# LRU stage with combined neighbour blocks and spread tiles, and a rebuilt first norm, first head and end

## What is computed

```python
h = rmsnorm(x, norm_mix)
q, k, v, g_ret, x_lru, y_lru, g_a, g_b = split(h @ w_in)
o, S_new = retention(rope(q), rope(k), v, S_ret)              # 4 heads, 256 x 512
ret_branch = (silu(g_ret) * groupnorm(o)) @ w_ret_out
xc = causal_conv(x_lru, conv_buf, conv_w, conv_b)             # width 1280, 4 taps
r, i = sigmoid(blockdiag(xc, w_a) + b_a), sigmoid(blockdiag(xc, w_x) + b_x)   # 16 blocks of 80
a = exp(-8 * r * softplus(-lam)); u = sqrt(1 - a * a) * i * xc
hl = scan(h = a * h + u)
lru_branch = (gelu(y_lru) * hl) @ w_lru_out
x = x + (sigmoid(g_a) * ret_branch + sigmoid(g_b) * lru_branch) @ w_o
x = x + (silu(h2 @ w_gate) * (h2 @ w_up)) @ w_down            # h2 = rmsnorm(x, norm_ffn), width 2816
```

## Time and profile before

| | |
|---|---|
| median of 3 runs | 2510.93 us (2508.16 to 2512.69) |
| profiled execution | 2510.63 us, its span 2508.8 us |
| TensorE busy | 2430.4 us, 97% |
| VectorE / ScalarE / GpSimd busy | 1191.4 / 606.9 / 1724.1 us |
| mean granted TensorE clock | 0.989 |
| moved by DMA | 298.6 MB, mean 119 GB/s |

### The profile page before, as it was taken

One profiled execution on the slowest core, in us unless ns is written; L12 is line 12 of the kernel. 1 busy time (PEld: TensorE's weight loads), 2 busy tenths in 40 slices (PEclk: granted clock), 3 DMA queues, 4 the chain that ended last, 5 costly groups with the idle time before them and its releaser, 6 DMA issues.

```text
span 2508.8 us, 53186 instructions
## 1 busy us (share of the span) xinstructions
PE 2430.4 (97%) x19604; PEld 2374.5 (95%) x19604; DVE 1191.4 (47%) x1613; ACT 606.9 (24%) x869; POOL 1724.1 (69%) x1993
## 2 busy tenths in 40 slices
PE   7999999999989999999989999999999899999997
PEld 7899999999989999999988999999999899999997
DVE  6554555477463532022256554545874645221223
ACT  2313121325361211011113132222353612100111
POOL 5365757488787877777754757565887777777774
PEclk9999999999999999999999999999999999999998
DMA  4445545422223222322235546352222332223222
GB/s 162 166 154 173 173 169 180 144 91 89 87 82 90 93 92 85 94 97 85 92 126 195 179 148 208 137 192 107 91 91 84 79 94 92 92 88 97 92 83 85
DMA packets 120224, 298.61 MB, mean 119 GB/s; under 512 B 19136, under 2 KB 19648, under 8 KB 120064
## 3 DMA queue, kind: packets, MB, share of 16 engines
q1 hardware_dynamic: 60480, 199.78, 24.8%
q10 hardware_dynamic: 59584, 96.56, 11.3%
HBM read 255.92 MB, written 40.38 MB: 118 GB/s over the span
## 4 chain that ended last, share of the span: by engine, by line
PE 86%; DVE 5%; ACT 2%; DMA 2%; issue 2%; DVEq 2%; ACTq 1%; POOL 0%; POOLq 0%; SPq 0%
PE banks L369 79%; PE banks L535 2%; PE banks L497 1%; DVE scratch L878 1%; PE banks L551 1%; PE banks L527 1%; DMA scratch<-in_sret 1%; DVE scratch L1080 1%; PE banks L514 1%; DMA w_raw<-in_wstream 1%; DVE rinv L697 0%; ACT scratch L1306 0%; DVE scratch L980 0%; DVE scratch L1062 0%; PE banks L454 0%
## 5 line engine op out<-in xcount | busy, mean ns | idle before, releaser
L355 POOL TENSOR_TENSOR w_low<-w_raw,w_high 128x256 fp32r<-128x256 f32 (+1 forms) x1568 | 1287.3, 852 | 62.2 <-issue 0.8
L350 POOL TENSOR_SCALAR w_high<-w_raw 128x1024 fp32r<-128x1024 f32 (+3 forms) x420 | 437.6, 1042 | 699.1 <-PE banks L369 671.0
L369 PE MATMUL banks<-x_high,w_high 128*128 128x260 f32 x4096 | 835.8, 285 | 44.8 <-DVE scratch L1102 15.6
L369 PE MATMUL banks<-x_high,w_low 128*128 128x260 f32 x4096 | 828.5, 284 | 0.0
L369 PE MATMUL banks<-x_low,w_high 128*128 128x260 f32 x4096 | 826.8, 284 | 0.0
L369 PEld LDWEIGHTS banks<-x_high,w_high 128*128 128x128 f32 x4096 | 635.4, 190 | 55.6 <-issue 47.2
L369 PE MATMUL banks<-split_scratch,w_high 128*128 128x260 f32 x4000 | 643.5, 283 | 5.4 <-DVE split_scratch L1091 5.4
L369 PEld LDWEIGHTS banks<-x_high,w_low 128*128 128x128 f32 x4096 | 634.7, 189 | 0.0
L369 PEld LDWEIGHTS banks<-x_low,w_high 128*128 128x128 f32 x4096 | 634.2, 189 | 0.0
L369 PEld LDWEIGHTS banks<-split_scratch,w_high 128*128 128x128 f32 x4000 | 548.9, 189 | 6.4 <-issue 6.0
L369 PE MATMUL banks<-split_scratch,w_low 128*128 128x260 f32 x2000 | 403.2, 283 | 0.0
(11 more groups left out here) (157 smaller groups left out, 1773.7 us busy)
## 6 DMA issues: line engine op xcount, KB each, us to landing
w_raw<-in_wstream SPq DMA_DIRECT2D x268, 512.0 KB, 3.5
scratch<-in_sret ACTq DMA_DIRECT2D x64, 512.0 KB, 7.3
out_ret_s<-scratch ACTq DMA_DIRECT2D x64, 512.0 KB, 3.4
w_raw<-in_wstream SPq DMA_DIRECT2D x64, 384.0 KB, 3.0
w_raw<-in_wstream SPq DMA_DIRECT2D x40, 448.0 KB, 3.2
scratch<-v_rows ACTq DMA_DIRECT2D x64, 256.0 KB, 4.5
w_raw<-in_wstream SPq DMA_DIRECT2D x48, 320.0 KB, 2.8
out_ret_p<-scratch ACTq DMA_DIRECT2D x8, 512.0 KB, 2.8
```

What stands on the lines that cost most here:

```text
L350: pool.tensor_scalar(WH[:, j, w], WR[:, j, w], 1.0, 0.0, ALU.mult, ALU.add)
L355: m = pool.tensor_tensor(WL[:, j, p], WR[:, j, p], WH[:, j, p].bitcast(F32), ALU.subtract)
L369: m = pe.matmul(out, wt[:, w, blk * P:(blk + 1) * P], x[xi], start=first and n == 0, stop=last and n == 2)
```

## The change

- Neighbour blocks: for an inner tile t the inputs of the upper half's neighbour (the lower half of tile t + 1) and of the lower half's neighbour (the upper half of t - 1) are copied into one tile XN (`neighbours`, ScalarE, four copies of 64 partitions), and the host combines the two weight blocks into one (`near`). A gate tile of t = 1, 2, 3 has 2 blocks in place of 3, and a y unit always 6.
- Second group: y(1,1) moves ahead of the 8 output tiles, y(1,2) into their middle; two more buffers for gated tiles (GLX); the orders of VectorE and ScalarE are written anew to match.
- First norm: X is loaded first, the gain is read from NRM, the square root's table is loaded at the start, ACC is cleared by GpSimd, all scalings and low parts stand ahead of half of the squares, and layer 0's norm sums come after the second tile. In each layer's first head the third tile goes into the fourth PSUM place.
- First head: `decays` in two parts, `conv_of_states` later, states and products earlier.
- The layer loop is unrolled on every engine; `norm_root` comes first in a layer; cos and sin of layer 1 are loaded after the last head of layer 0; the square root's table is loaded before the norm loops.
- End: the last norm makes no high and low parts, and its sums wait for the squares alone.

```diff
-YG_UNIT = [(MT + 2 * len(BAND[t])) // 2 for t in range(GT)]
...
+YG_UNIT = [(MT + 2 * 2) // 2] * GT
...
-             + [("y", 1, 0), ("ga", 0, GT)] + [("out", 0, m) for m in range(MT)]
-             + [("y", 1, t) for t in range(1, GT)] + [("ga", 0, m) for m in range(GT + 1, MT)])
+             + [("y", 1, 0), ("ga", 0, GT), ("y", 1, 1)] + [("out", 0, m) for m in range(MT // 2)]
+             + [("y", 1, 2)] + [("out", 0, m) for m in range(MT // 2, MT)]
+             + [("y", 1, 3), ("y", 1, 4)] + [("ga", 0, m) for m in range(GT + 1, MT)])
...
-            with sp.Fori(0, DEPTH) as layer:
+            for layer in range(DEPTH):
...
             pool.memset(ONES[:], 1.0).then_inc(s["ones_ok"], 1)
+            pool.memset(ACC[:], 0.0).then_inc(s["ones_ok"], 1)
...
                     if first:
                         whole(ub, 0, tb, 0, XH, XL, s["x_low_s"], layer * (2 * MT))
-                        norm_sums()
+                        if layer:
+                            norm_sums(2 * layer)
                         whole(ub, 1, tb, 1, XH, XL)
+                        if layer == 0:
+                            norm_sums(0)
                     else:
                         whole(ub, 0, tb, 0, XH, XL)
                         whole(ub, 1, tb, 1, XH, XL)
                         samples_by_channel(hh - 1)
                         for e in range(VT - 1):
                             out_by_channel(hh - 1, e)
-                    whole(ub, 2, tb, 2, XH, XL)
+
+                    whole(ub, KT, tb, KT, XH, XL, place=FIRST_K if first else None)
...
+                    q = spread(ub0, u, YG_UNIT[t], tb0, idx, [pairs(XH, XL, k) for k in range(MT)], 0)
+                    if t in INNER:
+                        n = g * len(INNER) + t - 1
+                        pe.wait_ge(s["xn_full"], layer * (GROUPS * len(INNER)) + (n + 1))
+                        xs = [pairs(XCH, XCL, t), pairs(XNH, XNL, n % 2)]
+                    else:
+                        pe.wait_ge(s["xc_low"], layer * LT + (g * GT + BAND[t][-1] + 1))
+                        xs = [pairs(XCH, XCL, k) for k in BAND[t]]
                     for w in range(2):
-                        q = spread(ub0, u, YG_UNIT[t], tb0, idx + 1 + w, XCH, XCL, BAND[t], q)
+                        q = spread(ub0, u, YG_UNIT[t], tb0, idx + 1 + w, xs, q)
...
                 y_gates(1, 0)
                 gate_a(GT)
+                y_gates(1, 1)
                 pe.wait_ge(s["gl_low"], layer * LT + GT)
-                for m_ in range(MT):
+                for m_ in range(MT // 2):
                     lru_out(ub0, B_OUT[m_], tb0, C_OUT[m_])
-                for t in range(1, GT):
-                    y_gates(1, t)
+                y_gates(1, 2)
+                for m_ in range(MT // 2, MT):
+                    lru_out(ub0, B_OUT[m_], tb0, C_OUT[m_])
+                y_gates(1, 3)
+                y_gates(1, 4)
                 for m_ in range(GT + 1, MT):
...
             for m in range(MT):
-                dve.wait_ge(s["x_high_s"], m + 1)
-                norm_low(X[:, m, :], XH[:, m, :], XL[:, m, :], GAIN[:, m:m + 1], m % 2, m == 0
-                         ).then_inc(s["x_low_s"], 1)
-                dve.drain()
-            with dve.Fori(0, DEPTH) as layer:
+                first_low(m)
+                if m > MT // 2:
+                    first_sum(m - MT // 2)
+            for m in range(MT // 2, MT):
+                first_sum(m)
+            dve.wait_ge(s["ones_ok"], 2)
+            dve.wait_ge(s["setup_ld"], 16 * 3)
+            for layer in range(DEPTH):
...
                     v_tile(1)
-                    if not first:
+                    if first:
+                        decays(0)
+                    else:
                         og_split(hh - 1)
                         dve.drain()
                     dve.tensor_copy(GNC[:], CUR[:, bass.ds(head * VT + PC_GN, VT)])
                     for e in range(2, VT):
                         v_tile(e)
-                        if first:
-                            (decays if e == 2 else conv_of_states)()
+                        if first and e == 2:
+                            decays(1)
                     aux(N_VS)
                     ts(OT[TT], AUX[:, BANK[N_VS], :], 1.0, None, ALU.mult).then_inc(aux_free[BANK[N_VS]], 1)
                     dve.drain().then_inc(s["vs_full"], 1)
+                    if first:
+                        conv_of_states()
                     if not first:
                         for m_ in range(MT):
...
                         dve.drain()
                         gate(0)
+                        new_state(1)
                     else:
                         score_low(0)
                         score_low(1)
...
                         k_low(i)
                     v_low(0)
                     if first:
-                        new_state(0)
+                        new_state(2)
                     gate(1)
                     for j in range(1, TT):
                         v_low(j)
                     if first:
-                        for n in range(1, SRING):
-                            new_state(n)
+                        new_state(3)
                     gate(2)
...
-                read_y(1, 0)
-                use_gates(1, 0)
                 scan(GT - 1)
                 conv_low(1, GT - 1)
                 gated_low(GT - 1)
+                read_y(1, 0)
+                use_gates(1, 0)
                 one_less_a2(GT)
                 use_ga(GT - 1)
                 read_ga(GT)
-                for m_ in range(MT):
-                    read_out(m_)
-                for t in range(1, GT):
-                    read_y(1, t)
-                    use_gates(1, t)
-                    scan(GT + t - 1)
-                    if t == 1:
-                        use_ga(GT)
-                    one_less_a2(GT + t)
-                    gated_low(GT + t - 1)
-                scan(LT - 1)
-                gated_low(LT - 1)
-                for m_ in range(GT + 1, MT):
-                    read_ga(m_)
-                for m_ in range(GT + 1, MT):
-                    use_ga(m_)
+
+                scan(GT)
+                gated_low(GT)
+                use_ga(GT)
+                read_y(1, 1)
+                use_gates(1, 1)
+                read_out(0)
+                one_less_a2(GT + 1)
+                read_out(1)
+
+                scan(GT + 1)
+                read_out(2)
+                gated_low(GT + 1)
+                read_out(3)
+                read_y(1, 2)
+                use_gates(1, 2)
+                read_out(4)
+                one_less_a2(GT + 2)
+                read_out(5)
+
+                scan(GT + 2)
+                read_out(6)
+                read_out(7)
+                gated_low(GT + 2)
+                read_y(1, 3)
+                use_gates(1, 3)
+                one_less_a2(GT + 3)
+
+                read_y(1, 4)
+                scan(GT + 3)
+                use_gates(1, 4)
+                one_less_a2(GT + 4)
+                read_ga(GT + 1)
+                gated_low(GT + 3)
+                scan(GT + 4)
+                gated_low(GT + 4)
+                read_ga(GT + 2)
+                use_ga(GT + 1)
+                use_ga(GT + 2)
...
+            def load_x(m):
+                act.dma_start(X[:, m, :], xt[:, m, :]).then_inc(x_ld[m], 16)
+
+            load_x(0)
+            act.dma_start(NRM[:], norms).then_inc(s["norm_ld"], 16)
+            for m in range(1, MT):
+                load_x(m)
+            act.wait_ge(s["boot"], 1)
+            A(TOUCH, EPST, ACT.Sqrt)
+            act.wait_ge(s["norm_ld"], 16)
+
+            def first_square(m):
+                A(SQ0[:, m, :] if m else SSQ, X[:, m, :], ACT.Square).then_inc(s["x_sq"], 1)
+
+            for m in range(MT):
+                act.wait_ge(x_ld[m], 16)
+                A(XH[:, m, :], X[:, m, :], copy, scale=NRM[:, 0, m:m + 1]).then_inc(s["x_high_s"], 1)
+                if m >= MT // 2:
+                    first_square(m - MT // 2)
+            for m in range(MT // 2, MT):
+                first_square(m)
+
...
                     if first:
+                        product(0)
+                        product(1)
                         silu(0)
                         for i in range(TT // 2):
                             k_high(i)
                         v_high(0)
-                        product(0)
-                        product(1)
-                        silu(1)
-                        for j in range(1, TT):
-                            v_high(j)
                         keep(0)
                         product(2)
                         keep(1)
                         product(3)
+                        silu(1)
+                        for j in range(1, TT):
+                            v_high(j)
                         keep(2)
                         keep(3)
                         product(4)
                         product(5)
                         silu(2)
```

(42 more changed lines are left out.)

208 lines of the change are left out of this document (121 added, 87 removed).

## The result

| | before | after |
|---|---|---|
| median | 2511.08 us (4 runs, 2508.16 to 2512.69) | 2468.35 us (4 runs, 2467.48 to 2471.05) |
| ratio | | 0.983, interval [0.9816, 0.985] |
| span of the profiled run | 2508.8 us | 2465.9 us |
| mean granted clock | 0.989 | 0.993 |

The change gains 42.7 us; 61.4 were forecast, and the time lies 0.35 us above the range of 2437 to 2468. The sign was right, the size was not.

What follows compares the result with a forecast made beforehand. TensorE, busy 97%, bounds the kernel; only fewer matmuls or holes help. Terms 3.0 + 30.2 + 6.8 + 5.8 + 6.8 + 7.2 + 1.6 = 61.4 us give 2449 us; forecast 2437 to 2458 (chance 0.70), outer bound 2468.

Steps and rivals of the forecast that it cites:

- What bounds, and the price of a hole: Whole kernel: TensorE's pace bounds, 0.72 us a block; a hole also slows the clock, 1.7 us for each.
- Fewer blocks and first group: LRU first group: 12 blocks fewer save 4.3 us a layer, less 2.8 for a new hole at y(0,1): net 1.5.
- Second group: LRU second group through merge: reordering y tiles and outputs gains 16.0 us in layer 0, 14.2 in layer 1.
- the 1.0 that I charged to GpSimd: LRU second group: 1.0 us charged for GpSimd's low pieces taking longer beside the chain, with one unit's lead.
- The stores: Merge: four small state stores beside it delay a weight load; 1.3 us charged (0 to 3).
- The heads: Loop over heads 1 to 3 in each layer: the prediction's sum held no term for it.
- The third rival: Unrolled layers: engines fetch new code, TensorE stalls 2.11 us at each fetch, some 25 a layer: 2555 us; chance 0.03.
- First norm: Kernel start: X loaded first, first matmul near 8 us, norm sums earlier; gain 6.8 us (3.5 to 9.5).
- First heads, layer change, end: First heads gain 5.8 and 6.8 us, the unrolled layer change 7.2, the last norm's sums 1.6.
- The chain (1): End of LRU second group: the ScalarE-VectorE chain still decides, holes of about 5 us a layer: 2459 us; chance 0.14.
- GpSimd (2): LRU second group: GpSimd becomes the bound, 11 us a layer: 2471 us; chance 0.08.

Runs made afterwards that it cites:

- the kernel with 20 waits: Kernel after with 20 already fulfilled TensorE waits (10 instructions) ahead of each layer's head loop: 2460.11 us, one execution.
- The run with 90 waits: Kernel after with 90 already fulfilled TensorE waits (45 instructions) ahead of each layer's head loop: 2452.47 us, one execution.
- The experiment: Kernel after with four of the residual's eight loads issued by ScalarE between its first splits: 2466.07 us, one execution.
- the run with three blocks: Kernel after plus 90 fulfilled waits ahead of each head loop, with inner tiles' gates made of three blocks again: 2467.98 us, one execution.
- heads written out: Kernel after with TensorE's loop over heads 1 to 3 written out in each layer: 2459.62 us, ratio to before 0.980.
- stores late: Kernel after with ScalarE's four small stores moved from ahead of merge to the feed-forward stage's start: 2457.35 us, ratio to before 0.979.
- both starts: Kernel after with four of eight residual loads issued by GpSimd (2471.86 us), or by ScalarE between its first splits (2466.07 us).
- 45 and 90 waits: Kernel after with 45 or 90 fulfilled TensorE waits (22 or 45 instructions) ahead of each head loop: 2454.6 and 2452.47 us.
- layer loop: Kernel after with only TensorE's two layers a loop again, layer 1's norm sums one tile later: 2462.9 us, ratio to before 0.981.

## Why the prediction was wrong

**What bounds, and the price of a hole.** It held: TensorE's pace, the block of 0.72 us, and that a hole is paid twice. But whether the clock falls is not the hole's size alone: 2.28 us at 555.67 brought half clock in after, and 2.29 us at 547.98 in the kernel with 20 waits did not. My 1.7 us each, or half of it, was a fair mean. The times of one kernel lie 2 to 7 us apart, and its executions with the longer times tend to show the lower mean clock. The run with 90 waits gained more than its holes for this reason.

**Fewer blocks and first group.** Right within about a microsecond. Four half-height copies start 0.65 us apart and not 0.54, so four take 2.6 us, the upper bound; a copy of 64 partitions takes 0.64 us, as long as one of 128. The hole was 2.28 us in layer 0, with half clock behind it, and 1.08 us in layer 1, with none, where 2.0 stood.

**Second group.** The hand-made order held: merge starts 91.7 us after y(1,0) where 91 was forecast. The hole of 1 to 2 us in the second output tile didn't come; instead TensorE waits for `w_low` (0.52, 0.30 and 0.41 us at 647, 677 and 697) and 0.10 at 665, 1.3 us together, near the 1.0 that I charged to GpSimd.

**The stores.** Here a term was mis-sized: 1.3 us a layer, against 6.1 and 4.3 us in the traces, 10.4 together, and 11.0 for both in the run without them there. I had the right row, 9.2 us for a load, and saw that the merge would now run at full speed beside it, but took the delay of the load for hidden by two buffers. I ought to have worked out the lead: the load of the earlier trace rows is some 6 us late, GpSimd comes from the second group with one unit of lead (3.6 to 4.3 us of TensorE's work), and the 2 us or more that are left bring half clock behind them. With the 10.4 us of the traces in the place of 2.6 the sum would have given 2457.

**The heads.** This is the step that failed: I gave the loop over the heads no term at all, and it cost 10.9 us, more than half of the miss. The third rival had the mechanism, that an engine without its next code stands for 2.1 us, but looked for it in the straight code, where no hole came, and argued from 550 to 650 us. The step not taken was to ask why one jump costs 2.11 us in the kernel before and the jump of the head loop nothing. For the head loop the answer is its place, and the change moves every place behind its first edit. Whether the layer loop's jump has a free place too, no run shows, since its target lay at the same place in all of them. The section named above of the Trainium skill has the rule; its blocks of 256 would have made the loop a rival of its own. By my estimate from the earlier trace rows that rival would have been 4 jumps of 2.1 us and two clock falls, some 12 us.

**First norm.** 5.5 instead of 6.8, within its bounds: the first matmul came at 9.49 us, not near 8. I let ScalarE's DMA issues pass in no time; nine take until 5.77 us, and the table load stands behind them. The experiment shows that with them out of the way the gains' own landing takes their place.

**First heads, layer change, end.** 20.4 us measured up to the change of layer and 2.1 at the end, against 19.8 and 1.6. Right, and for the reasons given: no hole before v's transposes in layer 0, none at the first tile of layer 1.

**The rivals.** The chain (1) no longer decides: no wait of TensorE for the read of a gate tile is left. GpSimd (2): it is busy 76.72 of 89 us in the second group, beside VectorE at 54.50, and TensorE misses 1.3 us:

```profile
640.00:729.00 89.00, 87.67 (x724) 86.92 (x723) 54.50 (x69) 62.43 (x77) 76.72 (x87) 1.00 0.28 87
```

The Trainium skill, "SBUF — State Buffer", section "SBUF: two separate sides", has GpSimd and a VectorE instruction with two SBUF inputs shut each other out for a whole instruction. These rows can't confirm or refute that, as a busy time may hold a wait for the other engine. The rival's time of 2471 us was close to the measured 2468, but by chance, since the 18.5 us were lost elsewhere and the run with three blocks gave GpSimd still more to do.

## What to carry to other kernels

Any edit that adds or removes instructions ahead of an engine's long loop may turn its jump from free to 3.0 us plus a slow clock, or back; look for holes with the releaser `issue` at the first instructions of a loop, and try a few dozen idle instructions ahead of it before anything else. Where a stage is made faster, ask what its slowness had covered: small scattered stores delayed a weight load by 3.4 to 6 us in each of the places seen here, so put them where the converting engine has a lead. And work out an engine's lead in microseconds before a delay is called hidden.

## What the runs showed of the hardware

- TensorE after the jump of its loop over heads: nothing, 1.0 to 1.8 us or 2.1 to 3.0 us, by the loop's place alone; ten instructions decide between 2.1 to 3.0 and none. Each hole goes with one more 16 KB packet on the queue of instructions, and the loop's code is loaded in every turn, 8 to 10 packets for 1939 recorded instructions.
- 422 fulfilled waits in a row, joined into 211 instructions, cost TensorE 18.63 us, 88 ns an instruction, where I had expected 30 to 50; 192 and 221 such instructions cost 82 to 89 ns each, and 45 only 0.6 us together. Why so few are nearly free is open.
- Beside four stores of 180 KB together in 4032 packets a weight load of 448 KB took 8.7 us (median 3.2) and one of 512 KB 6.9 us (median 3.5).
- Holes of 2.25 to 2.31 us at one and the same matmul, in y(0,1) of layer 0, had half clock behind them in five runs (after, heads written out, stores late, both starts) and none in four (20, 45 and 90 waits, layer loop).
- A ScalarE copy of 64 partitions x 520 takes 0.64 us, as one of 128 partitions.
